# Latent attention: softmax maxima as a step of their own, the next head's parts between them, and one weight tile split later

## What is computed

```python
def latent_attention(h, pos, w_in, q_norm, kv_norm, w_uq, w_ukv, q_gain, k_gain, w_out):
    c_q, c_kv, k_rope = jnp.split(h @ w_in, [256, 384], axis=-1)
    q = (rmsnorm_2(c_q, q_norm) @ w_uq).reshape(B, S, 16, 96)
    kv = (rmsnorm_2(c_kv, kv_norm) @ w_ukv).reshape(B, S, 16, 128)
    k_nope, v = jnp.split(kv, [64], axis=-1)
    k = concatenate([k_nope, broadcast(k_rope)])
    q, k = rmsnorm_2(q, q_gain), rmsnorm_2(k, k_gain)      # then rope on the last 32
    s = where(causal, einsum('bqhd,bshd->bhqs', q, k) * 96 ** -0.5, -1e30)
    o = einsum('bhqs,bshd->bqhd', softmax(s), v)
    return o.reshape(B, S, 1024) @ w_out
```

## Time and profile before

| | us |
|---|---|
| runs | 2663.80, 2663.81, 2667.22; median 2663.81 |
| the profiled execution | 2663.84 |
| its span in the trace | 2662.6 |
| PE busy | 2635.7 (99%) |
| PEld busy | 2210.8 (83%) |
| DVE busy | 1436.4 (54%) |
| ACT busy | 989.9 (37%) |
| POOL busy | 319.5 (12%) |
| chain that ended last: PE's share | 90% |
| chain that ended last: DVE, ACT, POOL | 3%, 3%, 2% |

### The profile page before, as it was taken

How to read it: one execution, slowest core, us unless ns; L and a number is a source line. 1 busy time by engine, 2 the same in 40 slices (tenths; PEclk the granted TensorE clock), 3 DMA queues, 4 the chain that set the end, 5 groups by cost and what they waited for, 6 DMA issues and landing times.

```text
span 2662.6 us, 31241 instructions
## 1 busy us (share of the span) xinstructions
PE 2635.7 (99%) x12738; PEld 2210.8 (83%) x12752; DVE 1436.4 (54%) x2266; ACT 989.9 (37%) x1650; POOL 319.5 (12%) x388
## 2 busy tenths in 40 slices
PE   9999999999999999999999999999999999999999
PEld 8898888888887788789988888888888788888887
DVE  7637547574757444356774343453434676543433
ACT  4344334342444222236642222322222586422221
POOL 0000010000021000015530000100000586200000
PEclk9999999999999999999999999999999999999999
DMA  5322325523223445464323332233232101233222
GB/s 161 119 88 90 101 80 177 167 80 111 79 95 95 107 103 103 94 112 104 107 95 106 96 100 87 87 111 95 95 95 78 62 22 38 91 110 96 95 91 68
DMA packets 278438, 258.92 MB, mean 97 GB/s; under 512 B 40324, under 2 KB 270743, under 8 KB 278295
## 3 DMA queue, kind: packets, MB, share of 16 engines
q1 hardware_dynamic: 278279, 256.93, 32.4%
q10 hardware_dynamic: 16, 0.00, 0.0%
HBM read 242.23 MB, written 14.68 MB: 96 GB/s over the span
## 4 chain that ended last, share of the span: by engine, by line
PE 90%; DVE 3%; ACT 3%; issue 2%; POOL 2%; DMA 0%; SPq 0%; POOLq 0%; DVEq 0%; ACTq 0%
PE bank L1183 29%; PE bank L1185 29%; PE bank L1184 29%; PE bank L1345 1%; POOL Wl L2489 1%; DVE Wl L1924 1%; ACT Wh L1557 0%; ACT Z L1847 0%; POOL TMP L2496 0%; PE bank L1409 0%; DVE Pl L2444 0%; PE bank L1282 0%; PE bank L1505 0%; DMA Z<-bias_scratch 0%; ACT Hh L1837 0%
## 5 line engine op out<-in xcount | busy, mean ns | idle before, releaser
L1183 PE MATMUL bank<-Hh,Wl 128*128 128x512 f32 x2136 | 838.4, 393 | 2.2 <-DVE Hl L1943 1.8
L1185 PE MATMUL bank<-Hh,Wh 128*128 128x512 f32 x2136 | 831.8, 389 | 0.0
L1184 PE MATMUL bank<-Hl,Wh 128*128 128x512 f32 x2136 | 831.5, 389 | 0.0
L1924 DVE TENSOR_TENSOR Wl<-RAW,Wh 128x1024 fp32r<-128x1024 f32 (+2 forms) x420 | 493.6, 1219 | 161.8 <-ACT Wh L1557 161.1
L1557 ACT ACTIVATE Wh<-RAW 128x1024 fp32r<-128x1024 f32 (+2 forms) x454 | 441.1, 1022 | 365.9 <-PE bank L1185 341.7
L1183 PEld LDWEIGHTS bank<-Hh,Wl 128*128 128x128 f32 x2136 | 401.1, 188 | 87.9 <-DVE Hl L1943 3.1
L1184 PEld LDWEIGHTS bank<-Hl,Wh 128*128 128x128 f32 x2136 | 401.1, 188 | 84.0 <-issue 1.7
L1185 PEld LDWEIGHTS bank<-Hh,Wh 128*128 128x128 f32 x2136 | 401.0, 188 | 83.8
L1183 PE MATMUL bank<-Ph,Wl 128*128 128x512 f32 x1152 | 452.0, 392 | 0.8 <-DVE Wl L1924 0.5
L1185 PE MATMUL bank<-Ph,Wh 128*128 128x512 f32 x1152 | 448.7, 389 | 0.0
L1184 PE MATMUL bank<-Pl,Wh 128*128 128x512 f32 x1152 | 448.3, 389 | 0.0
(11 more groups left out here) (336 smaller groups left out, 2501.1 us busy)
## 6 DMA issues: line engine op xcount, KB each, us to landing
RAW<-in_ffn_wg SPq DMA_DIRECT2D x44, 1024.0 KB, 5.3
RAW<-in_ffn_wu SPq DMA_DIRECT2D x44, 1024.0 KB, 5.3
RAW<-in_ffn_wd SPq DMA_DIRECT2D x32, 1024.0 KB, 5.1
RAW<-in_w_up SPq DMA_DIRECT2D x22, 1024.0 KB, 5.1
RAW<-in_w_in SPq DMA_DIRECT2D x20, 1024.0 KB, 5.2
RAW<-in_ffn_wd SPq DMA_DIRECT2D x16, 768.0 KB, 4.4
bias_scratch<-M SPq DMA_DIRECT2D x16, 512.0 KB, 8.2
RAW<-in_w_down SPq DMA_DIRECT2D x8, 1024.0 KB, 5.1
```

Source lines behind the costliest of these rows:

```text
L1183: mm(o, ll, rh, start=start, stop=False)
L1184: mm(o, lh, rl, start=False, stop=False)
L1185: return mm(o, lh, rh, start=False, stop=stop)
L1924: tt(Wl[:, n % 3, x:y], RAW[:, n % 2, x:y], f(Wh[:, n % 3, x:y]), ALU.subtract).then_inc(*w_lo.up(*([("w_lo", n)] if i else [])))
```

## The change

The maxima, which VectorE took in the step `b_scores`, are a step `b_max`. In a pass all three parts of `b_scores` come first, then for each part `b_max`; right behind `b_max` of part 0 stand now the two `b_qk` of the next head, and then the early exponential and the turn's low half. `b_attended` comes before the units. The tile for pairs 4 and 5 (the third of `bg`) is no longer split ahead when the second is taken in pass 0; a `split()` and a `load()` stand at the end of pass 2, behind `b_sum`. The sum of squares of unit (1, 0) is taken behind the copies of head 0's k and q.

```diff
--- before.py
+++ after.py
@@ -677,7 +677,7 @@
     ffn("s2", "glu", "b", "mix_norm_2", 8)
     norm_begin_rows("b")
     now["low"] = "pool"
-    attend_b_order(banks, tmps, next_tile, norm_step, hkeys, h_new, h_pair, stats, add_x, do)
+    attend_b_order(banks, tmps, next_tile, split, load, norm_step, hkeys, h_new, h_pair, stats, add_x, do)
     now["low"] = "dve"
     p_free("b_done", range(16))
     norm_begin("s3", "RF", (0, 2))
@@ -822,7 +822,7 @@
     out_units(32)
 
 
-def attend_b_order(banks, tmps, next_tile, norm_step, hkeys, h_new, h_pair, stats, add_x, do):
+def attend_b_order(banks, tmps, next_tile, split, load, norm_step, hkeys, h_new, h_pair, stats, add_x, do):
     do("b_begin")
     third = tmps.part(2)
 
@@ -850,7 +850,7 @@
 
     def unit(g, u, ring=None):
         if (u, g % 2) == (2, 0):
-            tile[g // 2] = next_tile("bg", g // 2, 1 if g else 0)
+            tile[g // 2] = next_tile("bg", g // 2, 1 if g > 2 else 0)
         (ring or banks).take(("b_u", g, u))
         tmps.take(("t_bu", g, u))
         do("b_unit", g, u, tile[g // 2])
@@ -902,6 +902,7 @@
     head_qk(0, 1)
     unit(1, 0)
     head_qk(0, 0)
+    do("b_unit_sum", 1, 0)
     unit(1, 1)
     do("b_scale", 1)
     rotate(1)
@@ -923,15 +924,16 @@
         for part in range(3) if i < 16 else ():
             scored.take(("b_s", i, part))
             do("b_scores", i, part)
+        for part in range(3) if i < 16 else ():
+            do("b_max", i, part)
             if part == 0:
+                for e in range(2) if i < 15 else ():
+                    head_qk(i + 1, e)
                 do("b_exp", i, 0)
                 if 0 <= t:
                     do("b_pt_lo", t, 1)
         if t in (14, 15):
             do("b_pt_lo", t, 1)
-        if i < 15:
-            for e in range(2):
-                head_qk(i + 1, e)
         if 0 <= t < 16:
             turned.take(("b_t", t, 2))
             do("b_turns", t, 2)
@@ -948,11 +950,14 @@
         if i < 16:
             do("b_exp", i, 1)
             do("b_sum", i)
+        if i == 2:
+            split()
+            load()
+        if v >= 0 and v % 2:
+            attended(v // 2)
         if 2 <= i < 12:
             for u in (0, 1) if i % 2 else (2, 3):
                 unit(g, u)
-        if v >= 0 and v % 2:
-            attended(v // 2)
         if i < 12 and i % 2:
             rotate(g)
             do("b_norm", g, 0, 16)
@@ -2378,7 +2383,7 @@
                 half = u % 2
                 at0 = 8 * (u // 2) + 4 * half
                 src = tmp(("t_bu", g, u))[:, 0:384 if u < 2 else 256].rearrange("p (m d) -> p m d", m=4)
-                if (g, u) in ((0, 0), (0, 1)) and kind == "b_unit":
+                if (g, u) in ((0, 0), (0, 1), (1, 0)) and kind == "b_unit":
                     continue
                 dve.wait_ge(*at(("b_usq", g, u)))
                 if g > 1:
@@ -2418,7 +2423,7 @@
                 dve.wait_ge(*at(("b_rot_products", g)))
                 tt(q[:, :, :, 64:80], t0[:, :, :, 0:16], t1, ALU.add)
                 tt(q[:, :, :, 80:96], t0[:, :, :, 16:32], t2, ALU.add).then_inc(*dve_out.up(("b_rot", g)))
-            elif kind == "b_scores":
+            elif kind == "b_max":
                 h, part = s
                 F, nm, E = fac[(h // 2) % 2], nmax[h % 2], EB[h % 3]
                 dve.wait_ge(*at(("b_F", h // 2)))
```

## The result

| | before | changed |
|---|---|---|
| median | 2666.54 us (6 runs) | 2675.19 us (6 runs) |
| lowest to highest | 2663.80 to 2667.22 | 2673.22 to 2676.24 |
| the profiled execution | 2663.84 | 2673.22 |
| its span | 2662.6 | 2672.0 |

The ratio is 1.0036, with an interval of 1.0026 to 1.0046: about 9.6 us slower (the medians are 8.65 apart, the profiled executions 9.4). The forecast was 2666.0 with a range up to 2671.0, counted from the profiled execution of before. In the changed file the engines' lines stand 5 further down: L2401 is L2406 (low copies of q and k), L2436 is L2441 (maxima), L2394 is L2399 (v's low half), L1837 is L1842 (high copies of q and k).

A forecast was written before the change was run, and what follows sets the result against it. TensorE was taken to lead by two microseconds only, with VectorE and ScalarE handing work to each other; pairs +2.0, splits +0.3 and third tile -0.2 made +2.1 on 2663.84: forecast 2666.0 us, range 2656.5 to 2671.

The forecast's parts named there:

- The pairs: Steps 4 to 11, an even and an odd head step each: +0.5 us a pair, +2.0 for four.
- the splits: ScalarE's weight halves in steps 4 and 8, no longer partly hidden: 0.15 us each, +0.3 in all.
- The bank: Odd steps: TensorE's last turns wait for a turn's low half, starting at 12.6 instead of 10.92, a new wait of 1.7.
- the rival of the clock: Step 9: a new TensorE wait of 2.7 us lowers the clock, uncovered, costing 3.3; total 2669.3 us, chance 0.25.
- steps 12 to 15: Head steps without units, where ScalarE catches up under an output unit on TensorE: costed at nothing.
- with 0.3 less it doesn't: Step 9: the clock falls only if TensorE's wait reaches 2.6 us; 0.3 less would not do it.
- The third tile and the first steps: Third weight tile's split moved from step 0 to the end of step 2: a gain of 0.2 us.
- Step 2's wait about 1 and full clock behind it: Step 2: TensorE's 2.6 us wait for GpSimd's scaling shrinks to about 1, with full clock after it.
- TensorE at step 3's transposes still waiting for GpSimd, near 2142: Step 3: a chain from a reciprocal through GpSimd, 2131.43 to 2142.16, still holds TensorE and swallows earlier gains.
- the moved split: End of step 2: no cost, the tile being first read in step 4, the loaded one split in step 8.
- before's low clock was hidden: After step 2's wait in the kernel before: clock 0.57 over 7.70 us, hidden under the chain to step 3's transposes.
- Faster, by busy shares: Rival: TensorE's 4.6 and 2.6 us waits simply go, other engines being 82% and 81% busy; 2656.6 us, chance 0.2.

The follow-up runs named there:

- filled: The change with dummy transposes of the identity in TensorE's waits of steps 2, 3, 5 and 9; ratio 1.0012 to the kernel before.
- qk_only: The kernel before with only the next head's q and k copies moved between the maxima; ratio 1.0025 to the kernel before.
- tile_back: The change with its third weight tile split again in pass 0, as in the kernel before; ratio 1.0028 to the kernel before.
- qk_odd: The kernel before with q's and k's copies behind the first maximum in odd steps 3 to 11 only; ratio 1.0001.
- q_odd: The kernel before with only q's copies behind the first maximum, in odd steps 3 to 11 only; ratio 0.9991.
- before_warm: The kernel before with 15 dummy transposes on TensorE ahead of the first turns of step 2; ratio 1.0001.
- low_last: The change with VectorE's low copies of q and k behind all three maxima, ScalarE's order unchanged; ratio 1.0001 to the kernel before.
- q_odd_tile_warm: q_odd with the change's tile move and moved sum, plus dummy transposes ahead of step 2's first turns and units; ratio 0.9989 to the kernel before.
- q_even: The kernel before with only q's copies behind the first maximum, in even steps 4 to 10 only; ratio 1.0022.

## Why the prediction was wrong

The step that failed is the clock behind the new waits. The forecast put it at nothing, and it cost 6.2 us. Steps 0 to 14 grew by 10.1 us where the forecast had 2.1; of the 8.0 between them the clock is 6.2 (3.3 of it in the first steps, where a gain of 0.2 was expected), an output unit 1.0, and the small rest is in the pairs and the first steps. The terms one by one:

**The pairs: right.** Forecast +0.5 a pair and 0.3 for the splits, +2.3 in all. With the clock held (filled), the four pairs grew by 0.58, 0.64, 0.58 and 0.82 (1.82 less the 1.00 of the output unit): 2.6. The splits don't show in it: the pairs with one (steps 4 and 5, 8 and 9) grew by 0.58, no more than the others. ScalarE's wait for the late maxima was 1.45, forecast 1.5; the last turns of step 7 start 12.80 after step 6, forecast 12.6.

**The bank: wrong, at no cost to the sum of the pairs.** I put the new wait at the last turns, for a turn's low half. It came earlier in TensorE's order, at the transposes, for v's low half (0.51 and 0.66). Before, v's second low half ended at 2175.30 and the transposes came at 2175.74, 0.44 of slack; the turn's low half ended at 2176.50 and the turns came at 2176.61, 0.11. Between the two low halves VectorE made that of the attended copy, which the change puts ahead of v's. In qk_only, where it isn't moved, the wait of step 7 is 0.45 at the transposes and 0.49 at the turns. The forecast looked at the turns' bank alone; the rival of the clock did look at the units' bank.

**The output unit: missed.** That steps 12 to 15 cost nothing holds (12 to 14 take 25.61 both times). But the first output unit is in step 11 and waits 1.00 us for a bank that ScalarE's late copies hold. It is there in the change, tile_back, qk_only, filled and qk_odd, in all of which both low copies go ahead of step 11's later maxima, and not in q_odd, where one does.

**The clock: the step that failed.** It was a rival, with a chance of 0.25, one place and 3.3 us, and the forecast had it at nothing. The waits were sized well: some 2.7 in step 9 and about 2.0 in step 5, measured 2.40 and 1.76. What failed is what they bring. The one in step 9 was to reach 2.6 us, and "with 0.3 less it doesn't"; it was 2.40, and the clock fell; it also fell after 1.27 and 1.76 us, in steps 3 and 5. It came three times, not once; the two in the pairs cost 1.55 (steps 4 and 5) and 1.34 (8 and 9), less than the 3.3 of one fall in the rival. I took the one wait that I could see ahead of a fall for the shortest that does it. The Trainium skill, TensorE: Matmul & The Clock Gate, section What's actually happening, halves the array's clock unless TensorE was busy of late. The trace agrees (0.72 over the 6.00 us behind each of the three waits), and filled shows the reverse, work of no use that keeps it up.

**The third tile and the first steps: wrong sign.** Forecast -0.2; steps 0 to 3 took 3.62 us longer. "Step 2's wait about 1 and full clock behind it": it was 1.64, with 0.85 behind it for a bank that ScalarE's square of a unit frees (L1818), and the clock was 0.57 all the same. "TensorE at step 3's transposes still waiting for GpSimd, near 2142": it waits there (2142.49), but for v's low half. In before that low clock was under cover. Here the eight transposes of step 2 run at low clock (1.91 us, 1.04 at full) and are waited for: ScalarE stands 2.23 us for them, VectorE 1.97 for ScalarE's high copy, then the late maxima, the exponentials, the moved split (1.35 on ScalarE) and v's copies all follow late, and the 1.27 us of wait bring the next fall. The prediction had the moved split at no cost; it asked when the tile is read, and not what stands behind the split on ScalarE in step 2. That before's low clock was hidden held (before_warm); that the change itself takes the cover away was not asked. Filled puts 3.3 of the 3.62 on the clock.

**The rivals.** Faster, by busy shares, fell: two engines at 82% and 81% set the end since they wait in turn. The Trainium skill, Perfetto Trace Analysis, section Identifying the Most-Contended Engine, says to optimise the engine with the highest occupancy first. Here that was no guide to the time: the change takes away TensorE's largest wait, and its waits above 0.2 us grew all the same, from 12.7 to 16.8 us in all, with neither of the others busier. The rival of the clock was the right mechanism, at half its size (3.3 against 6.2) and in one place of three. That its time, 2669.3, is nearer to the result than the forecast's is owed in part to a price for one fall that was twice too high.

Sum, from before's 130.73 to 140.87: pairs and splits 2.6, output unit 1.0, low clock 6.2, the rest of steps 0 to 3 0.3; together 10.1.

## What to carry to other kernels

Before a step is placed earlier, ask of each engine whether its input is there when that engine arrives: the same copy gained 0.7 us a pair where VectorE was behind its producer and lost 1.2 where it was ahead. When a forecast adds waits to TensorE, price the clock behind each of them, not only behind the longest; and when a loss is booked as hidden, ask whether the change moves its cover. For every bank or buffer that late work holds, read its slack: the first one in the engine's order takes the wait.

## What was not expected of the hardware

The granted clock fell after waits of 1.27, 1.76 and 2.40 us (and 0.45 more a group of transposes later) in steps where TensorE has no other wait above 0.3 us, and not after 0.51 and 0.66. In low_last, 1.15 and 0.43 in step 9 were enough (0.72 over 2197 to 2203), 0.50 and 0.43 in step 5 were not. The length of the wait doesn't settle it: in qk_only 1.29 and 0.45 in step 5 left the clock at 1.00 (2161 to 2169), and so did 1.48 in step 3 of q_odd_tile_warm (2141 to 2147). What else decides stays open. Each such fall cost about 1.7 us of TensorE's time. Dummy transposes of the identity, 128 columns each, in TensorE's waits kept the clock at 1.00 in filled.

The start of step 0 lay 4.6 us apart in the profiled executions of before and q_even, which are alike up to there. It goes with the low clock that q_even had on the way and before had not; why one execution has it there and another doesn't is open. The same holds for low_last, whose profiled execution shows 2.9 us more in the attention where its runs show none: its mean granted clock was 0.997, and the seven of its eleven executions with 0.999 took 2664.33 to 2665.74 us.
